# Latents' heads: ScalarE makes the convolution's middle tap, and ten row sets are used in the heads instead of at the end of the branches

## What is computed

```python
h = rmsnorm(x, norm_mix) * (1 + sc1) + sh1
proj = h @ w_in                                # q k v, z, gates, u, vg, ga, gb
qkv = silu(short_conv(qkv, conv_w))            # 3 taps over time, per channel
o = gated_delta(l2norm(q), l2norm(k), v, ...)  # both directions
p_a = (rmsnorm(o) * silu(z)) @ w_branch_a
p_b = (gelu(u) * (w_s @ rmsnorm(gelu(vg)) + b_s)) @ w_branch_b
x = x + gt1 * ((sigmoid(ga) * p_a + sigmoid(gb) * p_b) @ w_out)
h2 = rmsnorm(x, norm_ffn) * (1 + sc2) + sh2
# PEER: 8 heads pick 16 of 16384 experts each, so 128 experts per token
act = gelu(einsum('nd,ned->ne', h2, expert_u[ix]))
x = x + gt2 * einsum('ne,ned->nd', act * gates, expert_v[ix])
```

## Time and profile before

| | |
|---|---|
| median of 3 runs | 4622.6 us (4622.15 to 4629.96) |
| the profiled execution's own time | 4624.79 us, span 4623.0 us |
| PE busy | 4462.3 us, 97% of the span |
| DVE busy | 3094.3 us, 67% |
| ACT busy | 593.3 us, 13% |
| DMA | 1663.40 MB, mean 360 GB/s |

### The profile page before, as it was taken

One profiled execution on the slowest core, in us unless ns is written; L12 is line 12 of the kernel. 1 busy time (PEld: TensorE's weight loads), 2 busy tenths in 40 slices (PEclk: granted clock), 3 DMA queues, 4 the chain that ended last, 5 costly groups with the idle time before them and its releaser, 6 DMA issues.

```text
span 4623.0 us, 60331 instructions
## 1 busy us (share of the span) xinstructions
PE 4462.3 (97%) x25249; PEld 3285.4 (71%) x25249; DVE 3094.3 (67%) x4135; ACT 593.3 (13%) x1161; POOL 1482.4 (32%) x1047
## 2 busy tenths in 40 slices
PE   7989999999999998999999999999999999999997
PEld 2776446445885444466555445799999999999997
DVE  1455518897997774247777587978855558886556
ACT  1530001432431000000000010100000000000001
POOL 0110002673334643103544244433322223322221
PEclk8999999999999999999999999999999999999999
DMA  9939988995448989987999987599999999999998
GB/s 396 405 124 379 375 336 348 390 409 233 140 142 313 408 350 408 385 334 304 421 420 420 411 317 298 225 377 419 419 420 419 408 406 421 418 420 418 403 420 334
DMA packets 237322, 1663.40 MB, mean 360 GB/s; under 512 B 28230, under 2 KB 32728, under 8 KB 37786
## 3 DMA queue, kind: packets, MB, share of 16 engines
q0 software_dynamic: 129616, 936.57, 49.9%
q1 hardware_dynamic: 99348, 677.25, 36.6%
q10 hardware_dynamic: 8088, 45.73, 2.5%
HBM read 1639.68 MB, written 18.94 MB: 359 GB/s over the span
## 4 chain that ended last, share of the span: by engine, by line
PE 39%; DMA 8%; DVE 7%; issue 1%; POOL 1%; ACT 0%; ACTq 0%; DVEq 0%; POOLq 0%
PE ps L249 26%; PE ps L2737 12%; DMA arena_sb<-peer_v,arena_sb 7%; DVE arena_sb L447 3%; PE ps L2679 1%; POOL arena_sb L396 0%; DMA x_rows<-arena_sb 0%; DVE arena_sb L2426 0%; DVE arena_sb L2436 0%; DVE arena_sb L2428 0%; DVE arena_sb L2433 0%; DVE arena_sb L2423 0%; DVE arena_sb L2509 0%; DVE arena_sb L2464 0%; DVE arena_sb L2455 0%
## 5 line engine op out<-in xcount | busy, mean ns | idle before, releaser
L249 PE MATMUL ps<-arena_sb 128*128 128x224 f32 (+3 forms) x9728 | 2292.8, 396 | 8.4 <-ACT arena_sb L2237 2.6
L249 PEld LDWEIGHTS ps<-arena_sb 128*128 128x128 f32 x9728 | 1670.7, 192 | 614.2 <-issue 327.8
L447 DVE SCALAR_TENSOR_TENSOR arena_sb<-arena_sb 128x2048 f32<-128x2048 f32 x412 | 986.6, 2395 | 473.8 <-DMA arena_sb<-peer_v,arena_sb 442.9
L442 DVE CUSTOM_DVE_ANT_0 arena_sb<-arena_sb 128x2048 f32<-128x2048 f32 x416 | 975.5, 2359 | 326.7 <-DMA arena_sb<-peer_u,arena_sb 326.5
L396 POOL DMA_INDIRECT arena_sb<-peer_v,arena_sb x416 | 606.9, 1459 | 1135.6 <-DVE arena_sb L447 929.4
L396 POOL DMA_INDIRECT arena_sb<-peer_u,arena_sb x416 | 628.6, 1511 | 924.1 <-DVE arena_sb L442 571.6
L2737 PE MATMUL ps<-arena_sb 128*128 128x224 f32 x4096 | 776.5, 353 | 1.3 <-ACT arena_sb L2776 0.7
L2737 PEld LDWEIGHTS ps<-arena_sb 128*128 128x128 f32 x4096 | 774.4, 190 | 2.2 <-issue 1.0
L1949 PE MATMUL ps<-arena_sb 128*128 128x512 f32 x768 | 338.7, 599 | 15.0 <-DMA arena_sb<-w_gb_r 7.4
L1949 PEld LDWEIGHTS ps<-arena_sb 128*128 128x128 f32 x768 | 144.7, 191 | 203.4 <-issue 181.3
L2132 PE MATMUL ps<-arena_sb 128*128 128x512 f32 x640 | 275.8, 593 | 3.1 <-DMA arena_sb<-w_out 1.9
(11 more groups left out here) (329 smaller groups left out, 2871.4 us busy)
## 6 DMA issues: line engine op xcount, KB each, us to landing
arena_sb<-peer_ut SPq DMA_DIRECT2D x128, 1024.0 KB, 9.3
arena_sb<-peer_vt SPq DMA_DIRECT2D x128, 1024.0 KB, 9.3
arena_sb<-w_mod POOLq DMA_DIRECT2D x61, 1024.0 KB, 9.3
arena_sb<-w_qkv SPq DMA_DIRECT2D x48, 1024.0 KB, 9.2
arena_sb<-w_out SPq DMA_DIRECT2D x48, 1024.0 KB, 6.9
arena_sb<-w_query SPq DMA_DIRECT2D x48, 1024.0 KB, 7.1
arena_sb<-w_mod SPq DMA_DIRECT2D x35, 1024.0 KB, 8.9
arena_sb<-w_ga_r SPq DMA_DIRECT2D x32, 1024.0 KB, 8.4
```

The source lines that it names most:

```text
L249: mm = pe.matmul(out, weights[:, k * P:(k + 1) * P], x[:, k, :], start=(k == 0), stop=(k == chunks - 1))
L442: nc.vector.tensor_tensor_reduce(rows, rows, total, 1.0, 0.0, ALU.mult, ALU.add, seg.dots[:, p:p + 1]).then_inc(t.rows_used, 1)
L447: nc.vector.scalar_tensor_tensor(out=total, in0=rows, scalar=seg.weight[:, p:p + 1], in1=total, op0=ALU.mult, op1=ALU.add).then_inc(t.rows ...
```

## The change

DVE no longer makes the middle tap for the latents; ScalarE makes it as an activation (Copy, scaled by the tap's weight) at the head of each tile, before the root of the tile before. The two outer taps stay on DVE and wait for it through the same semaphore `conv_step`. The list of the heads becomes 5 behind each of the tiles 0 to 19 (100 sets), and the list of the u tiles 5, 5, 5, 5, 4, 0, 0, 0 (24). The DeltaNet's lists (35 sets) and those of z, vg and the merge keep their lengths, but each set number there is ten higher. The context's heads are as before.

```diff
@@ -798,7 +798,7 @@
     if ctx:
         behind = take(t, [0] * tiles, 6)
     else:
-        behind = take(t, [2] + [5, 4] * 3 + [5, 5, 4] * 4 + [5], 6) + take(t, [3, 2, 1, 0], 0, extra=(2, 3))
+        behind = take(t, [5] * 20, 6) + take(t, [3, 2, 1, 0], 0, extra=(2, 3))
         head_rows = behind[head.first - 1].stop
@@ -900,10 +900,10 @@
             w = [t.cw[:, n, k:k + 1] for k in range(3)]
-            tile_done(dve, t, n)
-
-            after(dve, silu_done, n - 1)
-            nc.vector.tensor_scalar(o, x, w[1], None, ALU.mult).then_inc(conv_step, 1)
+            if ctx:
+                tile_done(dve, t, n)
+                after(dve, silu_done, n - 1)
+                nc.vector.tensor_scalar(o, x, w[1], None, ALU.mult).then_inc(conv_step, 1)
             dve.wait_ge(conv_step, 2 * n + 1)
@@ -971,9 +971,19 @@
+        def conv_middle(n):
+
+            tile_done(act, t, n)
+            after(act, silu_done, n - 1)
+            after(act, conv_step, 2 * n)
+            nc.scalar.activation(y[n % 2], t.ps[:, n % 4, 0:nt], ACT.Copy,
+                                 scale=t.cw[:, n, 1:2]).then_inc(conv_step, 1)
+
         for n in range(tiles):
             if ctx and n % 4 == 0 and n:
                 mod_copy(act, nc, t, n // 4 - 1)
+            if not ctx:
+                conv_middle(n)
             if 1 <= n <= normed:
                 root(n - 1)
@@ -1591,7 +1601,7 @@
-    behind = take(t, [0] * (2 * H + 1) if ctx else [5, 4] * (H // 2) + [33] + [5] * (H - 2) + [4, 0], 4)
+    behind = take(t, [0] * (2 * H + 1) if ctx else [5, 4] * (H // 2) + [33] + [5] * 4 + [4, 0, 0, 0, 0], 4)
```

## The result

| | before | after |
|---|---|---|
| median, runs side by side on the same chips | 4627.8 us (22 runs, 4622.2 to 4636.4) | 4636.5 us (22 runs, 4624.3 to 4648.3) |
| ratio of the times, 95% interval | | 1.0018 [1.0011, 1.0025]: 8.3 us slower [5.1, 11.6] |
| the profiled execution's own time, span | 4624.79, 4623.0 us | 4642.18, 4640.3 us |

The change makes the kernel 0.18% slower, where 4623.5 us, 0.8 us above before, was forecast. The median of 4636.5 us lies 2.5 us above the range's upper end of 4634. The more telling comparison is that of the differences: the range allowed for -10.6 to +11.4 us around the 4622.6 us of three runs of before, the 22 runs of before have their median 5.2 us higher, and the difference itself is +8.3 instead of +0.8.

A forecast was written before the change was run, and what follows sets the result against it. PE, busy 97% of the span, was taken to bound the kernel. Heads +16, merge -15.5 and renumbering +0.3 gave +0.8 us on a 4622.6 us median, called 4623.5 us; range 4612 to 4634 us.

The forecast's parts named there:

- Part 1: Heads: the middle tap leaves DVE, 19.0 us less there, none on PE's path; DVE can carry five sets each tile.
- Part 2: Heads: the tap on ScalarE takes 15.6 us, costed at 0; only tile 20's outer taps start 1.0 us later.
- rival (d): Heads: the tap doesn't free DVE, 14.6 us per tile stay; 4625 us, sharing 0.68 with the forecast.
- Part 3: Heads: ten more sets make the last set 14 us late; cost 16 us, bounds 13 and 24.
- one idle time of PE of about 12 us before L708: End of the heads: PE, ready at 1091.2, stands 12.3 us for DVE's differences, where today it doesn't.
- The clock's 2 us: Heads, tile 22: after PE's idle time 5 to 9 us run at half speed; 2 us taken as lost.
- Part 4: Merge: ten sets fewer behind the u tiles leave fewer waits for weights; gain 15.5 us, bounds 11 and 17.7.
- Rival (c): Merge: its stalls are its own, so the gain is only 5 us; sum +11.3, 4634 us, chance 0.08.
- the ring: Merge's start: four weight tiles held ready, 13.9 us of cover; with three queues sharing, used up at 1787 us.
- Part 5: DeltaNet: renumbering makes ten more sets adds, about 0.05 us longer each; 0 to 0.5 us, taken as 0.3.
- (a): Heads: DVE, not the queue, sets the pace; heads end 3 us later, total -12.2, 4610.5 us, chance 0.12.
- (b): Heads: spare transfer time can't be used, POOL asks up to 1.9 us later; +12.7, 4635.5 us, chance 0.12.

The follow-up runs named there:

- e2: The kernel before with only the two new lists (100 sets in the heads, 24 behind u), tap on DVE; -2.3 us [-7.4, 2.8] against before.
- e1: The kernel before with only the middle tap moved to ScalarE, both lists as before; +1.4 us [-2.8, 6.0] against before.
- e3: The change with ScalarE making tile 7's middle tap ahead of the gates' four activations; +2.8 us [-2.8, 7.9] against before.
- e4: The change with DVE's two gate products made ahead of tile 7's sets instead of behind; -0.9 us [-5.6, 4.2] against before.
- e10: As e6, but h is stored only when all 106 sets of the heads are used; -1.4 us [-6.5, 3.2] against before.
- e13: The change with 28 sets behind vg instead of 33 and 29 behind u instead of 24; +14.4 us [8.8, 19.9] against before.
- e12: As e8, but four sets moved from the u to the z tiles (40 behind z, 25 behind u); -2.3 us [-6.9, 2.3] against before.
- e8: As e6, but five sets moved instead of ten (95 in the heads, 29 behind u); -8.8 us [-13.0, -4.6] against before.
- e9: The kernel before with only five sets moved (95 in the heads, 29 behind u), tap on DVE; -8.8 us [-14.4, -2.8] against before.
- e5: The change with the 3 MB of h stored only after the last set behind tile 19; +6.0 us [1.9, 10.2] against before.
- e7: The change with the edits of e3, e4 and e5 together; -1.9 us [-6.9, 3.2] against before.
- e6: As e2 (tap on DVE), with the edits of e4 and e5 added; -0.9 us [-5.6, 3.2] against before.

## Why the prediction was wrong

The likeliest mechanism (transfers moved from one full place to another) was right, and it also holds on the gain's side. Two things were left out: what the tap has to queue behind on ScalarE, and a second place where PE needs something of DVE's.

**Part 1** (19 us less on DVE): its size is right, DVE has 17.7 us less busy time in all. That it is not on PE's path is right too. The conclusion that DVE can carry five sets a tile thanks to it was beside the point: e2 keeps the tap on DVE, and its last set ends 4.2 us earlier than the change's.

**Part 2** (the tap on ScalarE, costed at 0 but for tile 20) is the first step that failed. The duration was right (0.67 us for 0.65), and so was tile 20: DVE's L908 waits 1.67 us for it, in the change as in e1. What I asked was who waits for ScalarE's root behind the tap, and for POOL, which gathers behind its product, I charged nothing; in e1 its gathers come 2 us later. I did not ask what stands in front of the tap. Behind tile 6 that is four activations of the gates, which wait for DVE. It costs 3.5 us of the heads (e3); the other 1.7 (e3 against e2) hold tile 20, where the outer taps start 1.67 us behind the last set instead of 0.70, 1.0 us later as forecast. With the lists of 90, 95 and 100 sets the tap made the heads 2.3, 4.9 and 5.2 us longer. By the forecast's own rival (d), "it stands in ScalarE's order behind what DVE itself is late for", I had the mechanism, but priced it as no loss.

**Part 3** (the last set 14 us late, one stand, +16): the transfers' arithmetic holds. Where the first stand is taken away (e4), the last set is 12.9 us later than before from the heads' start; the forecast was 14, from the lower bound of 13.0. The failed step is the "one idle time of PE of about 12 us before L708". PE needs a thing of DVE's at tile 8 too, L949 behind tile 7's sets, with a slack of 0.4 us that can be read in the trace of before, though no wait stands there. Because of it the stand splits, the clock falls twice (6.4 us instead of the forecast 2), and the transfers have a hole 23 us behind the stand: 71.5 us at 374 instead of 421 GB/s are 8.0 us of transfers, and the last set comes 20.6 us late, just beyond the upper bound of 19.9. That e2's heads give +16.1 where +16 was forecast is a coincidence: two stands of 5 us are not one of 12.3. The clock's 2 us came from rows 10, whose first window (0.70) holds the idle time itself, so it was a weak base.

**Part 4** (-15.5, bounds 11 and 17.7): right, -14.4 in the change and -11.4 to -15.9 in the seven other runs with 24 sets and 33 behind vg. The remaining DMA waits are 0.9 + 0.8 + 0.7 + 0.3 = 2.7 us, forecast 2.2. Rival (c) is out. Two small slips stand in the prediction: rows 8 show two full windows ahead of the merge's, not three; and the ring "used up at 1787 us" counts its 13.9 us as if no tile landed in that time. In the change PE first waits for a weight tile 14 us after the merge's start, for 0.4 us.

**Part 5** (+0.3): the DeltaNet takes 300.8 to 306.7 us in the runs other than e10, and 302.8 in e13, whose sets are numbered as in the change. So the +3.3 of the profiled execution isn't the renumbering's. A term of 0.3 can't be seen in this scatter.

**The sum** would have been +21.3 - 14.4 = +6.9, with an estimated 1 us at the mix +8, and +8.3 was measured. Against the forecast of +0.8, the tap on ScalarE makes 5.2 us of the difference in the heads, the merge 1.1, and the sets almost nothing (16.1 for 16). The tap's cost, put at 0, is thus the term that moved the total. Over all kernels, heads and merge together give the ratio of the times to within 5 us, but for e10 and e12, whose loss lies in the DeltaNet and at the mix.

**The rivals.** (a) had DVE as the bound: out, by e1 and e2. (b) said that the spare can't be used and gave +12.7: right in part. Its delay of POOL is seen in e1. But in the change the spare is used from 792 us on, and some of it is lost again behind a stand, not through the sum of squares from tile 16 on. **The signs:** "the heads' windows all at about 421 GB/s" failed at 898.8 to 970.3, and "if PE stands within tiles 1 to 16" is what happened. The last set's end at 1101.0 us lies in the window of 1095 to 1102 by luck: the heads began 1.7 us earlier than before, and counted from there it is 0.7 us outside.

## What to carry to other kernels

Before more work is put on an engine that runs beside the critical one, list every place where the critical engine takes something from it, and read the slack at each from the two timelines: a place without a wait may have 0.4 us. An instruction moved to an idle engine inherits whatever stands in front of it there, and that engine's idle time may be a wait for the very engine that was to be relieved. Spare transfer time is used up with a kink: five sets cost 0 to 2.2 us in the heads and gave 9 in the merge (e8, e9), ten cost 16 and gave 14 (e2).

## What the runs showed that I had not expected

- A store counts like a load. The 3 MB store of h beside the last sets delayed them by 7.5 us in the change (against e5); 3.1 MB at 421 GB/s are 7.5. Two more pairs, in which the tap or the gate products move as well, give 7.1 and 7.9 (e4 and e7, e9 and e8).
- A stand of PE costs again in the clock, and not in proportion. After 3.38 us of idle time (e6, L708) the sixteen matmuls take 3.79 us instead of 1.95 and the tile behind them 15.03 instead of 13.90; after 7.48 us (the change) they take 3.78 and 14.38. After 0.37 us (e5) they take 2.05 and 13.90. That is the level of 1.2 GHz for the small matmuls and the beginning of the tile.
- The engines that move the data pay for a stand of PE, but later. Weight tiles and sets are asked for by finished work, so in the change a stand of 7.1 us, itself at 421 GB/s, was followed by 8.0 us of lost transfers (162 GB/s from 930 to 940 us), and by the second stand.
